# Wide expert items of a mixture-of-experts layer: the rest rows' products, eviction and scatter behind those of the main rows

## The reference

```python
def swiglu(x, w_gate, w_up, w_down):
    return (jax.nn.silu(x @ w_gate) * (x @ w_up)) @ w_down
...
    def expert_block(acc, blk):
        e, rows, g = blk
        yb = swiglu(x2[rows], w_gate[e], w_up[e], w_down[e])
        return acc.at[rows].add(yb * g[:, None].astype(x2.dtype)), None
```

## Time and profile before

| | |
|---|---|
| median of 3 runs | 2029.44 us (2026.68 to 2031.22) |
| the profiled execution | 2032.41 us, span 2030.7 us |
| PE busy | 1951.9 us (96% of the span) |
| DVE, ACT, POOL busy | 1120.6, 769.2, 545.0 us |
| granted TensorE clock, mean | 0.986 |
| first and last start of the rest rows' products | 1182.9 and 1651.7 us |
| last eviction of `y_main` starts | 1991.1 us |

### The profile page before, as it was taken

The page is one execution under the profiler, slowest core; times in us unless marked ns, Lnnn a source line. Parts: engine busy times, 40 slices in busy tenths (PEclk is TensorE's granted clock), DMA queues, the critical chain, the costliest instruction groups (busy, mean ns, idle before and its releaser), DMA issues. The chain is left out here.

```text
span 2030.7 us, 38892 instructions
## 1 busy us (share of the span) xinstructions
PE 1951.9 (96%) x12777; PEld 1692.9 (83%) x12777; DVE 1120.6 (55%) x3394; ACT 769.2 (38%) x1504; POOL 545.0 (27%) x892
## 2 busy tenths in 40 slices
PE   8999999999999999999999999999999999999992
PEld 8778889888988778888787788988888889998981
DVE  6735563565366543232667755555555566666655
ACT  3424551554244531112444033334344343433334
POOL 7365565000022300000100133433344432222210
PEclk9999999999999999999999999999999999999996
DMA  5522212212334421110431599999999999999994
GB/s 169 118 78 56 81 48 73 64 48 63 89 102 121 127 63 52 41 52 11 161 104 63 197 346 309 310 326 322 316 325 324 324 350 365 371 361 339 341 350 173
DMA packets 174481, 382.57 MB, mean 188 GB/s; under 512 B 24878, under 2 KB 115798, under 8 KB 148784
## 3 DMA queue, kind: packets, MB, share of 16 engines
q1 hardware_dynamic: 148432, 314.11, 42.9%
q0 software_dynamic: 25376, 67.16, 14.5%
q10 hardware_dynamic: 576, 0.05, 0.0%
HBM read 328.85 MB, written 63.67 MB: 193 GB/s over the span
## 5 line engine op out<-in xcount | busy, mean ns | idle before, releaser
L2722 PE MATMUL ps_gu<-xe,w_raw 128*128 128x136 f32 (+6 forms) x4224 | 513.7, 282 | 2.9 <-DMA w_raw<-in_exp_w_gate 1.5
L2722 PEld LDWEIGHTS ps_gu<-xe,w_raw 128*128 128x128 f32 x4224 | 502.0, 191 | 3.7 <-DMA w_raw<-in_exp_w_up 1.8
L2675 POOL DMA_INDIRECT scr_acc<-y_main,out_idx x66 | 102.6, 1554 | 298.3 <-DMA scr_acc<-y_main,out_idx 139.2
L1190 ACT ACTIVATE w_raw_first<-w_raw_first,o_stage 128x128 f32<-128x128 f32 (+1 forms) x192 | 86.4, 450 | 199.5 <-DVE o_stage L1136 198.7
L2825 DVE TENSOR_TENSOR w_lo<-w_raw,w_hi 128x1024 fp32r<-128x1024 f32 x132 | 155.2, 1217 | 1.3 <-ACT w_hi L2768 1.3
L2768 ACT ACTIVATE w_hi<-w_raw 128x1024 fp32r<-128x1024 f32 x132 | 132.1, 1049 | 39.1 <-DMA w_raw<-in_exp_w_down 38.9
L2796 ACT ACTIVATE y_main<-ps_ye,gate 128x512 f32<-128x512 f32 (+2 forms) x132 | 90.9, 688 | 118.6 <-PE ps_ye L92 118.5
L2669 POOL DMA_INDIRECT scr_acc<-y_rest,out_idx x36 | 64.4, 1788 | 213.1 <-ACT y_rest L2793 213.1
L2848 DVE TENSOR_TENSOR e_h<-e_silu,ps_gu 128x128 f32<-128x128 f32 (+6 forms) x132 | 38.2, 289 | 148.7 <-PE ps_gu L2722 148.6
L2783 ACT ACTIVATE e_silu<-ps_gu 128x128 f32<-128x128 f32 (+6 forms) x132 | 37.0, 281 | 212.3 <-PE ps_gu L2722 184.4
L90 PE MATMUL ps_ye<-w_hi,e_h_hi 128*128 128x512 f32 (+2 forms) x264 | 110.2, 418 | 0.4 <-DVE e_h_lo L2852 0.2
(11 more groups left out here) (507 smaller groups left out, 4680.5 us busy)
## 6 DMA issues: line engine op xcount, KB each, us to landing
w_raw<-in_exp_w_gate SPq DMA_DIRECT2D x66, 1024.0 KB
w_raw<-in_exp_w_up SPq DMA_DIRECT2D x66, 1024.0 KB
w_raw<-in_exp_w_down SPq DMA_DIRECT2D x66, 1024.0 KB
w_raw_first<-in_w_in SPq DMA_DIRECT2D x24, 512.0 KB
v_w_raw<-in_w_in SPq DMA_DIRECT2D x48, 256.0 KB
scr_att<-o_stage SPq DMA_DIRECT2D x16, 264.0 KB, 3.0
att_prev<-scr_att SPq DMA_DIRECT2D x16, 264.0 KB, 4.0
merged<-in_x_cols SPq DMA_DIRECT2D x8, 512.0 KB, 9.6
```

The source lines that it names most:

```text
L1190: act.activation(probs[:, w % 2, 0:n], probs[:, w % 2, 0:n], ACT.Exp, scale=-1.0, bias=o_stage[:, blk, at + 1:at + 2], accum_out=o_stage[: ...
L2675: pool.indirect_dma_start(out=acc_rows[0], out_offset=bass.IndirectOffsetOnAxis(ap=out_idx[j][0:rows, 0:1], axis=0), in_=y_main[j][0:rows, ...
L2722: ins = pe.matmul(ps_gu[:, 2 * w + c, 0:width], w3(raw[j][w])[:, k, P * c:P * c + P], xT[:, k, 0:width], start=(k == 0), stop=(k == KD - 1))
```

## The change

In each wide item, on three engines, the block for the rest rows is moved behind the block for the main rows. Nothing is added or removed, and the waits go with their blocks. SP's and DVE's instructions stay as they are. The semaphores are signalled by the same instructions as before.

```diff
@@ POOL, turn @@
                     if width > P:
                         hold(rest_out[1 - j], 16 * (pair + j))
-                        hold(rest_evac, n + 1)
-                        pool.indirect_dma_start(out=acc_rows[1], ... in_=y_rest[j][:, :], ...).then_inc(rest_out[j], 16)
                     if width == P and j == 0:
                         hold(rest_out[1], 16 * rests)
                     hold(y_evac, 2 * n + 2)
                     pool.indirect_dma_start(out=acc_rows[0], ... in_=y_main[j][0:rows, :], ...).then_inc(scattered[j], 16)
+                    if width > P:
+                        hold(rest_evac, n + 1)
+                        pool.indirect_dma_start(out=acc_rows[1], ... in_=y_rest[j][:, :], ...).then_inc(rest_out[j], 16)
@@ PE, turn @@
                     pe.wait_ge(y_evac, 2 * n)
+                    pe.wait_ge(lo_made, 2 * n + 2)
+                    for half in range(2):
+                        cols = slice(512 * half, 512 * half + 512)
+                        for c in range(2):
+                            if half == 0:
+                                pe.wait_ge(h_made, 2 * n + c + 1)
+                            ins = mm3(pe, ps_y[0:rows, half, :], ..., c == 0, c == 1)
+                        ins.then_inc(y_done, 1)
                     if width > P:
                         pe.wait_ge(h_ready, 2 * n + 2)
                         pe.wait_ge(ld[j][DOWN], 16 * (pair + 1))
                         pe.wait_ge(rest_evac, n)
                         for c in range(2):
                             for q in range(4):
                                 ins = pe.matmul(ps_y[REST * q:REST * q + width - P, 2, 0:QD], h[:, c, P:width], ...)
                         ins.then_inc(rest_done, 1)
-                    pe.wait_ge(lo_made, 2 * n + 2)
-                    for half in range(2):
-                        ... (the same block)
@@ ACT, turn @@
                     act.wait_ge(scattered[j], 16 * pair)
+                    for half in range(2):
+                        act.wait_ge(y_done, 2 * n + half + 1)
+                        act.activation(y_main[j][0:rows, 512 * half:512 * half + 512], ...).then_inc(y_evac, 1)
                     if width > P:
                         act.wait_ge(rest_out[j], 16 * pair)
                         act.wait_ge(rest_done, n + 1)
                         act.activation(y_rest[j][:, :], ps_y[:, 2, 0:QD], ...).then_inc(rest_evac, 1)
-                    for half in range(2):
-                        ... (the same block)
```

More of the change, by code:

```diff
@@ L2667, in turn @@
                         hold(rest_out[1 - j], 16 * (pair + j))
-                        hold(rest_evac, n + 1)
-                        pool.indirect_dma_start(out=acc_rows[1], out_offset=bass.IndirectOffsetOnAxis(ap=out_idx[j][:, 1:2], axis=0),
-                                                in_=y_rest[j][:, :], in_offset=None, bounds_check=4 * L - 1, oob_is_err=False,
-                                                compute_op=ALU.add).then_inc(rest_out[j], 16)
                     if width == P and j == 0:
@@ L2677, in turn @@
                                             compute_op=ALU.add).then_inc(scattered[j], 16)
+                    if width > P:
+                        hold(rest_evac, n + 1)
+                        pool.indirect_dma_start(out=acc_rows[1], out_offset=bass.IndirectOffsetOnAxis(ap=out_idx[j][:, 1:2], axis=0),
+                                                in_=y_rest[j][:, :], in_offset=None, bounds_check=4 * L - 1, oob_is_err=False,
+                                                compute_op=ALU.add).then_inc(rest_out[j], 16)
                 for s in range(4):
@@ L2729, in turn @@
                     pe.wait_ge(y_evac, 2 * n)
+                    pe.wait_ge(lo_made, 2 * n + 2)
[4 more added lines that the diff above has]
+                                pe.wait_ge(h_made, 2 * n + c + 1)
+                            ins = mm3(pe, ps_y[0:rows, half, :], h_hi[:, c, 0:rows], h_lo[:, c, 0:rows],
+                                      d3(hi[j][:, :])[:, c, cols], d3(lo[j][:, :])[:, c, cols], c == 0, c == 1)
+                        ins.then_inc(y_done, 1)
                     if width > P:
@@ L2789, in turn @@
                     act.wait_ge(scattered[j], 16 * pair)
+                    for half in range(2):
+                        act.wait_ge(y_done, 2 * n + half + 1)
+                        act.activation(y_main[j][0:rows, 512 * half:512 * half + 512], ps_y[0:rows, half, :], ACT.Copy,
+                                       scale=gate[j][0:rows, 0:1]).then_inc(y_evac, 1)
                     if width > P:
@@ L2793, in turn @@
                         act.activation(y_rest[j][:, :], ps_y[:, 2, 0:QD], ACT.Copy, scale=gate[j][:, 1:2]).then_inc(rest_evac, 1)
-                    for half in range(2):
-                        act.wait_ge(y_done, 2 * n + half + 1)
-                        act.activation(y_main[j][0:rows, 512 * half:512 * half + 512], ps_y[0:rows, half, :], ACT.Copy,
-                                       scale=gate[j][0:rows, 0:1]).then_inc(y_evac, 1)
                 act.wait_ge(turned, 2)
```

## The result

Over 20 executions of each kernel on one chip, the changed kernel takes 2035.2 us (2029.0 to 2047.5) against 2029.2 us (2025.5 to 2034.8): ratio 1.0034, interval 1.0024 to 1.0044. It is slower by 6 us at the medians, by 7 according to the ratio, where 4 us less were forecast. The profiled execution took 2032.36 us, span 2030.6, and lies 2.8 under its median.

What follows compares the result with a forecast made beforehand. PE alone was taken to set the pace in wide items; 3.84 us instead of 3.95 saves 0.11 an item, 4.0 over 36 items, so 2029.4 - 4.0 = 2025.4 us, range 2019.5 to 2032.5.

Steps and rivals of the forecast that it cites:

- The change on PE: PE, wide items, transposes to index sums: 3.84 us instead of 3.95, 0.11 less an item, 4.0 in all.
- the seam main to rest: PE, between main rows' and rest rows' products: a gap not shown in the trace, taken as 0.09 us.
- The first main pass: PE: should start within 0.03 us of the transposes' end, with the second pass 0.31 to 0.34 behind.
- ACT and `w_down`: ACT: load goes out 2.76 us later; total wait grows to between 50 and 100 us, off the path.
- The second rival: Late `w_down` load slowed beside the main scatter, ACT late, PE stalls: 27 us net slower, 2056 us; chance 0.08.
- POOL: POOL's queue: main scatter about 1 us earlier, rest scatter behind it, gathers about 1 us later, at no cost.
- The bound: Wide items: PE, busy 100.00 of 100 us, alone sets the pace; other engines matter only if PE waits.
- The Trainium skill: DMA engines alternate between queues by packets: a scatter under way slows a load but does not stop it.
- The first rival: PE's seams cost the same in either order: no change, 0 +- 1.8 us, 2029.4 us; chance 0.18.
- the waits in front of the index sums: Sign of error on PE: waits before the index sums would mean ACT's copies come late.
- PE's wait for `e_h_lo`: Sign of error: PE waiting at the second half of the hidden values; 0.68 us was left there.
- lost cover: The rest rows' block covered DVE's second half of hidden values; after the move 0.68 us was said to remain.

Runs made afterwards that it cites:

- e9: The changed kernel with rest rows added into other memory, so the next main scatter need not wait for their landing (output wrong): 2027.4 us, ratio 0.9985.
- e10: The changed kernel with rest rows' products reading only the high part of `w_down`, so its load goes out early (low part missing): 2025.8 us, ratio 0.9987.
- e3: The kernel before, with SP in wide items also waiting for the main rows' products before loading `w_down`: 2032.4 us, ratio 1.0005.
- e8: The change only in the 13 items wider than 144, the old order elsewhere: 2028.2 us, ratio 1.000 against the kernel before.
- e7: The kernel before, with each wide item loading 0.13 MB more behind its gate weights, read by nobody: 2030.3 us, ratio 0.9998.
- e5: The changed kernel, with wide items' gate and up loads bringing 112 of 128 partitions (output wrong): 2041.6 us, ratio 1.005.
- e6: The kernel before, with wide items' gate and up loads bringing 112 of 128 partitions (output wrong): 2046.6 us, ratio 1.0092.

## Why the prediction was wrong

*The change on PE*: right. 3.84 us were forecast for the stretch and 3.82 measured; the seam main to rest was taken as 0.09 and is 0.09. The first main pass starts 0.08 us before the end reckoned for the transposes (1316.56 against 1316.64), not within 0.03 of it, and the second 0.31 behind the first, as said. Where nothing stalls (e9, e10), the wide stage takes 464.3 to 464.4 us instead of 468.8: 4.4 to 4.5 us over 35 distances, 0.13 each, against 0.11 forecast.

*ACT and `w_down`*: right in size and in its harmlessness. 50 to 100 us of waits were forecast, 86.4 came; SP's wait for the rest rows' products grew too, from 63.4 to 168.4 us. The second rival put the loss there; e9 has 92.7 us of that wait and no loss.

*POOL* is the step that failed. "the main scatter moves from 1314.09 to about 1313.0 ... Queued behind it are the two gathers ... so 1 us costs nothing": this follows what is queued *behind* the scatters and never asks who waits for their *landing*. Two do, POOL before its next scatter and DVE before it copies the indices. In the changed kernel POOL waits 188.2 us in 25 items for a landing, and the wide stage takes 472.3 us instead of some 465. The gathers behind came not 1 us late but late enough for PE to wait 1.29 us for one. The prediction did state that the load would go out half a microsecond ahead of the main scatter and share the engines with it, and had both landings at hand, 6.6 and 10.1 us. It used the difference only against the load and never put it into the chain. With the earlier trace rows: main scatter at 1314.09, landing at 1320.7, one microsecond to the next scatter, against the next rest scatter 13.8 us after 1311.03 (or 13.4, the average item of the earlier trace rows), at 1324.4 to 1324.8: about 3 us to spare. Less the 3.5 between the two landings of the earlier trace rows, nothing is left. The rows were there.

The bound was misread for the same reason: "PE alone sets the pace" was true of the busy share (100.00 of 100 us), but a chain of about 10.7 us ran beside it against 13.4, and the change lengthened that one to 13.1.

*The Trainium skill*, "DMA: Bandwidth & Descriptors", "Queues, rings and completion order": the rule that each DMA engine takes turns between its queues by packets was cited there with "the sum is the same without this". Read with it, the traces say that the effect goes both ways: with the load beside it a scatter is slower too, 9.3 us instead of 6.6 in the undisturbed items of e3, and that was the direction that counted.

*The first rival* (seams cost the same) is refuted by the 0.13 us; the waits in front of the index sums, named as a sign of error, did not come. Of what was named as a sign of error, PE's wait for `e_h_lo` came, at the second half of the hidden values (eight times, up to 0.4 us) as at the first (seven times, up to 0.9), and for another reason: not lost cover, for no undisturbed item shows it, but DVE held up by the landing.

Open: what sets off the first late item. It differs between executions of one program (e3: 2 of 12, e8: 2 of 11, once also an execution of the kernel before, 2045.8 us of a median of 2030.6), and no trace here shows the moment as caused by any one instruction.

## What to carry to other kernels

For each transfer that a change moves, or beside which it puts another, list not only what is queued behind it but every wait on its completion, and write down the loop: issue, landing, wait, next issue. Compare that loop's length with the item's; if a few microseconds of slower landing close the gap, the change can cost more than it saves, and the busy shares will not show it. Where a load's release moves, look at what it will run beside before looking at who needs it.

## What the runs showed that was not expected

- A loop through shared DMA engines can hold two states: in e8 the same scatter lands after 6.4 us when issued on time and after 11.4 when issued late, for fourteen items on end.
- A load that starts 2.8 us later draws out transfers of another queue by 2.7 us (e3, items in which nothing stalls: 9.3 against 6.6), while 3% more bytes, with the `w_down` load where it was, draw them out by 0.9 (e7: 7.5 against 6.6).
- A 112-partition load, 896 KB, keeps the DMA engines longer than one of 128 partitions and 1024 KB. With the changed order, the plain loads take 66.7% of their time for 85.10 MB (e5) against 63.1% for 94.22 (the changed kernel); with the order before, 66.7% for 84.56 (e6) against 57.4% for 94.51, but there e6 stalls and the other doesn't.
